# A compression network in a two-block transformer step: windows standing, weights moving, and its place behind two score steps

## What is computed

```python
kcc = compress_tokens(kc, pe[0], w1[0], b1[0], w2[0], b2[0])   # 15 windows of 32 tokens, 4 heads
vcc = compress_tokens(vc, pe[1], w1[1], b1[1], w2[1], b2[1])   # gelu(xb @ w1 + b1) @ w2 + b2
o_cmp = compressed_attention(q, kcc, vcc)       # 15 keys
o_sel = selected_block_attention(q, ks, vs, ...)  # at 256 tokens: all causal keys
o_win = banded_attention(q, kw, vw, 512, None)
o = g0 * o_cmp + g1 * o_sel + g2 * o_win ; y = o @ w_out
```

## Time and profile before

| what | time |
|---|---|
| median of 3 runs | 1802.1 us (1791.11 to 1802.98) |
| the profiled execution | 1789.85 us |
| its span (first to last instruction) | 1787.6 us |
| end of nsa_v to start of out2 | 1156.57 to 1261.03 us |

### The profile page before, as it was taken

The page is one execution under the profiler, slowest core; times in us unless marked ns, Lnnn a source line. Parts: engine busy times, 40 slices in busy tenths (PEclk is TensorE's granted clock), DMA queues, the critical chain, the costliest instruction groups (busy, mean ns, idle before and its releaser), DMA issues.

```text
span 1787.6 us, 32466 instructions
## 1 busy us (share of the span) xinstructions
PE 1694.1 (95%) x11348; PEld 1520.5 (85%) x11348; DVE 1216.1 (68%) x2234; ACT 916.6 (51%) x1749; POOL 565.1 (32%) x230
## 2 busy tenths in 40 slices
PE   2997999999999999999999999989899999799998
PEld 1985899999999998788888878976799999589997
DVE  5467509779718993878887758639578877646665
ACT  2445444455469994454545454247544445554443
POOL 0780377989975455000000007320210004130000
PEclk8899899999999999999999999969999998989999
DMA  8665455556653335888888655343568764136663
GB/s 324 224 207 169 144 177 176 178 185 178 185 168 118 113 111 183 326 283 291 293 290 285 195 165 149 120 150 126 165 224 282 281 224 133 34 107 188 188 187 107
DMA packets 98568, 341.14 MB, mean 191 GB/s; under 512 B 12290, under 2 KB 16146, under 8 KB 98482
## 3 DMA queue, kind: packets, MB, share of 16 engines
q1 hardware_dynamic: 94130, 336.01, 56.9%
q10 hardware_dynamic: 4352, 4.02, 0.8%
HBM read 337.87 MB, written 1.07 MB: 190 GB/s over the span
## 4 chain that ended last, share of the span: by engine, by line
PE 87%; DVE 5%; ACT 3%; DMA 3%; issue 2%; ACTq 0%; SPq 0%; DVEq 0%
PE banks L611 25%; PE banks L612 25%; PE banks L613 25%; PE banks L890 3%; DMA arena<-in_ada 2%; DVE arena L1546 1%; PE banks L1054 1%; PE banks L776 1%; DMA ada_ring<-in_ada 1%; PE banks L750 1%; PE banks L682 1%; PE banks L789 1%; DVE arena L1653 1%; PE banks L675 1%; DVE negmax L1632 1%
## 5 line engine op out<-in xcount | busy, mean ns | idle before, releaser
L564 POOL TENSOR_TENSOR weights_low<-ring,weights_high 128x1024 fp32r<-128x1024 f32 x226 | 564.9, 2512 | 1041.1 <-DVE ht_low L1621 625.9
L1167 ACT ACTIVATE weights_high<-ring 128x1024 fp32r<-128x1024 f32 x480 | 505.2, 1054 | 510.1 <-PE banks L613 481.2
L611 PE MATMUL banks<-ht_high,weights_high 128*128 128x256 f32 x2008 | 582.5, 290 | 8.5 <-DVE ht_low L1621 6.0
L612 PE MATMUL banks<-ht_low,weights_high 128*128 128x256 f32 x2008 | 572.2, 285 | 0.0
L613 PE MATMUL banks<-ht_high,weights_low 128*128 128x256 f32 x2008 | 572.0, 285 | 0.0
L611 PEld LDWEIGHTS banks<-ht_high,weights_high 128*128 128x128 f32 x2008 | 389.5, 194 | 14.2 <-issue 11.4
L612 PEld LDWEIGHTS banks<-ht_low,weights_high 128*128 128x128 f32 x2008 | 389.7, 194 | 2.7
L613 PEld LDWEIGHTS banks<-ht_high,weights_low 128*128 128x128 f32 x2008 | 389.1, 194 | 0.0
L1601 DVE TENSOR_TENSOR weights_low<-ring,weights_high 128x1024 fp32r<-128x1024 f32 x254 | 310.5, 1223 | 40.2 <-ACT weights_high L1167 34.5
L611 PE MATMUL banks<-weights_high,ga_parts 128*128 128x512 f32 x504 | 197.7, 392 | 5.8 <-DVE ga_parts L1903 5.8
L612 PE MATMUL banks<-weights_low,ga_parts 128*128 128x512 f32 x504 | 197.0, 391 | 0.0
(11 more groups left out here) (249 smaller groups left out, 2328.8 us busy)
## 6 DMA issues: line engine op xcount, KB each, us to landing
ring<-in_stream SPq DMA_DIRECT2D x490, 512.0 KB, 3.6
arena<-in_ada SPq DMA_DIRECT2D x88, 512.0 KB, 4.1
ada_ring<-in_ada SPq DMA_DIRECT2D x56, 512.0 KB, 4.3
arena<-bias_rows ACTq DMA_DIRECT2D x1, 2048.0 KB, 13.4
X<-in_x SPq DMA_DIRECT2D x1, 1024.0 KB, 5.8
out<-X SPq DMA_DIRECT2D x4, 256.0 KB, 2.0
arena<-arena ACTq DMA_DIRECT2D x8, 127.5 KB, 4.9
arena<-in_norm_final SPq DMA_DIRECT2D x1, 512.0 KB, 4.6
```

Of the source, the lines that this page charges most:

```text
L564: pool.tensor_tensor(WL[:, c % SLOTS, :], ring[:, c % SLOTS, :], WH[:, c % HIGHS, :], ALU.subtract)\
L611: pe.matmul(out, wh, xh, start=start, stop=False, **kw)
L612: pe.matmul(out, wh, xl, start=False, stop=False, **kw)
L1167: act.activation(WH[:, c % HIGHS, :], ring[:, c % SLOTS, :], ACT.Copy).then_inc(S["high_ready"], 1)
```

## The change

1. Phi's first layer is turned round: 60 window columns are stationary, 256 columns of `w1` move. Keys write partitions 0 to 59 and values partitions 64 to 123 of bank 7, alternately. The weights are reordered on the host so that a chunk holds 4 rows-of-128 with 256 columns each, keys and values in turn.
2. The bias is now a row, added by two matmuls with a row of ones. The gelu (60 x 256, twice) leaves hidden units on the free axis, so 4 transposes and one VectorE copy turn them back before the second layer.
3. Phi's first layer stands behind the scores of steps 0 and 1, the transposes behind step 0's, the second layer behind step 1's. In group 0 both "cmp" steps are moved behind the other four.
4. nsa_v goes to banks 6 and 7, out of the way of the scores; the gates on VectorE come after the windows.
5. SyncE loads the 8 chunks of out2 between ada pieces 1 to 8, no longer ahead of all of them; ScalarE's `high` of the first four stands in the last four attention steps (20 to 23), no longer right behind phi. The `low` of each on GpSimd follows.

```diff
-        att2 = plan(lambda g: ["sel", "win", "cmp"], 8, 8)
+        att2 = plan(lambda g: ["sel", "win", "cmp"], 8, 8, lambda s: (s["g"], s["g"] == 0 and s["last"]))
...
-            load_chunks(ahead + SLOTS, chunk["out2"] + SLOTS)
+            load_chunks(ahead + SLOTS, chunk["out2"])
...
+                if 1 <= i <= SLOTS:
+                    load_chunk(chunk["out2"] + i - 1)
...
+                if kind == "cmp":
+                    pe.wait_ge(S["cmp_taken"], 2)
...
+            def phi_hidden():
+                pe.wait_ge(S["windows_ready"], 4)
+                pe.wait_ge(S["phi_loaded"], 16 * 7)
+                pe.wait_ge(S["vv_taken"], 2)
+                for q in range(4):
+                    c = chunk["phi"] + 2 * q
+                    for kv in range(2):
+                        arrived(c + kv)
+                    for l in range(4):
+                        for kv in range(2):
+                            m = pe.matmul(banks[window_rows[kv], 7, 0:T], WIN[:, kv, 4 * q + l, :],
+                                          ring[:, (c + kv) % SLOTS, l * T:(l + 1) * T], start=q == 0 and l == 0, stop=False,
+                                          skip_group_check=True)
+                            if l == 3:
+                                m.then_inc(S["chunk_used"], 1)
+                pe.wait_ge(S["ones_row_ready"], 1)
+                for kv in range(2):
+                    m = pe.matmul(banks[window_rows[kv], 7, 0:T], ones_row[0:1, 0:60], A(A_B1R, 2, T)[0:1, kv, :],
+                                  start=False, stop=True, skip_group_check=True)
+                m.then_inc(S["phi_done"], 1)
+
+            def phi_turned():
+                pe.wait_ge(S["hid_ready"], 2)
+                for kv in range(2):
+                    r = window_rows[kv]
+                    if kv:
+                        pe.wait_ge(S["hid_turned"], 1)
+                    for mm in range(2):
+                        m = pe.transpose(banks[:, 7, T + (2 * kv + mm) * 60:T + (2 * kv + mm + 1) * 60],
+                                         HIDT[r, mm * P:(mm + 1) * P], ident[r, r])
+                    m.then_inc(S["hid_turned"], 1)
...
-            pe.wait_ge(S["gate_taken"], 1)
-            for kv in range(2):
-                pe.wait_ge(S["windows_ready"], 2 * (kv + 1))
...
-            attention(att2, keys2, lambda s, h: Q2[:, h // 2, :], vals2)
+            attention(att2, keys2, lambda s, h: Q2[:, h // 2, :], vals2, {-1: phi_hidden, 0: phi_turned, 1: phi_out})
...
+            def take_hidden(i):
+                if i == 1:
+                    act.wait_ge(S["phi_done"], 1)
+                    for r in window_rows:
+                        act.activation(HIDT[r, :], banks[r, 7, 0:T], ACT.Gelu_apprx_tanh).then_inc(S["hid_ready"], 1)
...
+            def beside_att2(i):
+                if i == 2:
+                    act.wait_ge(S["cmp_ready"], 1)
...
+                if i >= len(att2) - HIGHS:
+                    used(chunk["phi"] + 8 + i - len(att2))
...
+                if step == 1:
+                    dve.wait_ge(S["hid_turned"], 2)
+                    dve.tensor_copy(A(A_HID, 240), banks[:, 7, T:T + 240]).then_inc(S["hid_taken"], 1)
```

More of the change, by code:

```diff
@@ L793, in values, with attention @@
                 m.then_inc(S["values_done"], 1)
-            def attention(steps, keys, queries, vals):
+            def attention(steps, keys, queries, vals, beside={}):
                 for s in steps[:2]:
                     scores(s, keys, queries)
+                if -1 in beside:
+                    beside[-1]()
                 for i, s in enumerate(steps):
@@ L804, in attention @@
                     probs_transpose(s)
+                    if i in beside:
+                        beside[i]()
                 values(steps[-1], vals)
@@ L1036, in _ @@
             m.then_inc(S["gate_ready"], 1)
+            pe.wait_ge(S["out_taken"], OUTS["nsa"] + 16)
+            deep("nsa_v", 4, 512, per=2, bank=6)
+            def phi_hidden():
[18 more added lines that the diff above has]
+                m.then_inc(S["phi_done"], 1)
@@ new lines, in phi_out @@
+            def phi_out():
+                pe.wait_ge(S["hid_taken"], 1)
+                for mm in range(2):
+                    m = pe.matmul(banks[:, 7, 0:60], A(A_W2D, 2, P)[:, mm, :], HID[:, mm, :], start=mm == 0, stop=mm == 1)
+                for g in range(4):
+                    o = banks[0:N_CMP, 7, T + g * HD:T + (g + 1) * HD]
+                    for mm in range(2):
+                        pe.matmul(o, HID[:, 2 + mm, g * N_CMP:(g + 1) * N_CMP], A(A_W2, 2, 2, HD)[:, 1, mm, :],
+                                  start=mm == 0, stop=False)
+                    m = pe.matmul(o, ones[0:1, 0:N_CMP], A(A_B2V, HD)[0:1, :], start=False, stop=True)
+                m.then_inc(S["cmp_ready"], 1)
@@ L1230, in take_values, with attention @@
                     .then_inc(S["y_high_ready"], 1)
-            def attention(steps):
+            def attention(steps, first=lambda i: None, beside=lambda i: None):
                 exps(steps[0])
                 for i, s in enumerate(steps):
+                    first(i)
                     if i:
                         take_probs(steps[i - 1])
+                    beside(i)
                     if i > 1 and steps[i - 2]["last"]:
@@ L1678, in _ @@
             dve.memset(epsc[:], EPS).then_inc(S["eps_ready"], 1)
+            dve.memset(ones_row[:], 1.0).then_inc(S["ones_row_ready"], 1)
             dve.memset(one_of[:], 0.0).then_inc(S["one_ready"], 1)
```

76 lines of the change are left out of this document (22 added, 54 removed).

## The result

The changed kernel takes 1778.63 us (median of 13 runs, 1773.12 to 1785.98); the kernel before, run beside it, 1794.09 (13 runs, 1790.12 to 1802.98). The ratio is 0.9915 with an interval of 0.9900 to 0.9929, so the gain is 12.7 to 17.9 us, 15.5 by the medians. The forecast was 1781.5 us and a gain of 20.6. The time is 2.9 us from it, and that is partly luck: the 1802.1 us that it started from lay 8.0 us above the median of before that 13 runs give, and the gain was put 5.1 us too high, so the two errors took each other away in part. The forecast gave 0.55 to a gain beyond 1%; it came out at 0.85%, for which it had 0.40. The profiled executions are 1789.85 and 1779.83 us.

What follows compares the result with a forecast made beforehand. TensorE was busy 95% of the span, but VectorE's start and pace on the attention were taken to count. Gain 22.1 - 1.5 = 20.6 us from a median of 1802.1 gave 1781.5 us; range 1767 to 1793.

Steps and rivals of the forecast that it cites:

- a: Ahead of phi: two score steps of 128 keys take 2.0 us, so phi begins at 1158.5.
- b: Phi's first layer: halves run beside each other, 0.47 us a pair, 8.0 us in all; bounds 7.3 and 14.6.
- rival 1: Phi's first layer: the halves do not overlap, 14.6 us instead of 8.0; gain 14.0, time 1788.1; chance 0.13.
- rival 3: Small bare costs: phi's weight loads (3.4 us) or pauses at both table loads (2.6); gain 17.2 or 18.0; chance 0.08.
- c: From phi's end to group 1's first maxima: a chain of 16.3 us, gaining 22.1 us up to there.
- rival 2: Start is a chain at TensorE's lower clock, or the tail costs more: 8 us lost, gain 12.6; chance 0.20.
- d: The rest of the attention, from group 1 to out2, stays as it was at 56.1 us.
- e: The tail, steps 20 to 23: the moved `high` and `low` cost 1.5 us; bounds 0 and 13.1.
- f: Moved nsa_v banks, rotary wait, gates, bias row and out2's chunks cost nothing; 3.5 us once if cover were gone.
- Rival 4: Slower: phi at the lower clock without overlap takes 29.2 us, group 0 loses 8; time 1810.7; chance 0.04.

Runs made afterwards that it cites:

- fed kernel of before: The kernel before with 10 idle bf16 matmuls while TensorE waits for the gelu between phi's keys and values: 1787.74 us, ratio 0.9960.
- fed steps: The changed kernel with 2 idle bf16 matmuls in each attention step ahead of the wait for the probabilities: 1779.36 us, ratio 0.9927.
- filled run: The changed kernel with lows on VectorE, idle matmuls in attention steps and more in the last ones: 1776.18 us; with early highs and lows: 1777.46 us.
- phi first: The changed kernel with phi's first layer ahead of the two score steps: 1784.85 us, ratio 0.9950 to the kernel before.
- highs behind: The changed kernel with the four `high` behind the exponentials (steps 19 to 22) instead of ahead: 1779.67 us, ratio 0.9916.
- both of these: The changed kernel with the four `low` on VectorE and the four `high` behind the exponentials: 1785.11 us, ratio 0.9949.
- after again: The changed kernel run once more for a second profile, nothing edited: one run, 1774.4 us.
- halves apart: The changed kernel with phi's matmuls as four on the keys' partitions, then four on the values', not in turn: 1776.17 us, ratio 0.9908.

## Why the prediction was right, and where it was wrong

a. *Two score steps ahead*: 1.95 us for 2.0. Right. The place itself was worth 6 us with what hangs on it.

b. *Phi's first layer*: 7.7 us for 8.0 (1162.03 to 1169.73 with the bias). Mechanism and size were right: the two halves run beside each other, a pair of matmuls costs 0.43 us, and the 0.04 that I added to each pair from the values' row is not there. So rival 1 is answered by the trace: one half alone takes 0.43 us a matmul, and 32 of them one behind the other would be 13.8 us by that figure, hardly less than the 14.5 of before at the full clock (2 x 7.25). So turning the operands round pays here because it lets two halves be used, not by itself. (Before, 60 moving columns took 0.227 us a matmul, with the weight loads busy for 7.11 us beside 7.25 of matmuls; whether the loads set that pace no run shows.) Neither small cost of rival 3 was there: the loads lie under the matmuls, and no pause stands ahead of or behind the bare table load.

c. *From phi to group 1*: forecast 26.2 us behind nsa_v, measured 27.13, 25.86 again, 28.5 in four profiles of the same start, and 25.24 with the clock held. The sum of the chain fits; the clock's part was left out, up to 3.3 us. So rival 2's first half happened, at a quarter to four tenths of its price of 8. I had forecast a clock of 1.0 up to group 1; in the first profile it fell to 0.50 for 7 us or so ahead of it.

d. *The rest unchanged*: wrong by 1.7 us, plus 1.5 of clock in the first profile. Group 1 takes 18.35 to 18.57 us at a clock of 1.00 in three runs with the new order, and 16.89 in the fed kernel of before. The fed steps show where, in VectorE's timeline at the start of group 1:

```profile
1183.71 0.18 DVE L1683 RECIPROCAL rsum<-sums 128x4 f32<-128x4 f32 x1 [0.41 <-ACT arena L1238]
1185.58 0.69 DVE L1668 TENSOR_REDUCE negmax<-banks 128x4 f32<-128x512 f32 x1 [0.81 <-PE banks L768]
```

VectorE waits 0.41 us for exponentials and 0.81 for the next scores, so the second maxima come 2.97 us behind the first (1182.61); before it was 1.55 (1204.90 to 1206.45), with no wait. Both "cmp" steps of group 0 now stand right ahead of this place. That they are short and leave VectorE less to do while the others work is argued, as no run undid that order alone.

e. *The tail* is the step that failed: forecast 1.5 us, measured 4.9 in the first profile and 3.6 in the second. The mechanisms named are there. GpSimd holds VectorE up, in VectorE's timeline after:

```profile
1234.60 2.62 DVE L1684 TENSOR_SCALAR arena<-arena,rsum 128x15 f32<-128x15 f32 x4
1241.91 1.31 DVE L1682 TENSOR_TENSOR rsum<-rsum,arena 128x4 f32<-128x4 f32 x1
```

and in TensorE's, what it waits for, and how the last values run:

```profile
1237.27 1.03 PE L784 MATMUL banks<-const,arena 128*15 128x128 f32 x4 [2.52 <-DVE arena L1684]
1243.54 1.97 PE L797 MATMUL banks<-arena 128*64 128x128 f32 x16 [1.11 <-ACT arena L1247]
```

But four `high` and four `low` there cost 0.9 us once the clock is held and the lows are VectorE's. The other 4.0 and 2.7 are the clock and GpSimd's meetings with VectorE; how they share is not shown, as no filled run left the lows on GpSimd. What there is points to the clock as the larger part: it stood at 0.50 in a part of every tail that was not filled, in both orders, and taking the lows from GpSimd without holding the clock left the tail at 26.6 us. Rival 2 had named it ("the tail costs more"). What I left out is that the profile of before held a short such fall (0.92 over its last group) which another execution of nearly the same kernel had long (0.73, 25.62 us). Whether the new order makes it fall more often than the old is open: with one profile of each kernel I can't tell, and it may be that the true loss in e is nearer to the forecast than to 4.9.

f. *At nothing*: VectorE waited for one ada piece, 0.32 us under phi where it waited afterwards anyway, and phi did not wait for its chunks. Right.

So: forecast 22.1 - 1.5 = 20.6; in the first profile 21.20 - 3.14 - 4.94 = 13.12, in the second 22.47 - 1.73 - 3.62 = 17.12, and 12.7 to 17.9 by the runs. Of its own list of what would make it wrong one thing came, in both profiles: the last group over 26 us. Rival 4 didn't come: phi ran at 1.00. Two small slips of its sums changed nothing: the top of the range takes 10 us of gain for rival 2, which is put at 12.6 elsewhere, and 9 us of TensorE's work at the lower clock would cost 9, not about 8. The later start of the stage (3.5 us) can't be put down to the change: nsa_v ends anywhere from 1157.4 to 1163.9 in the profiles of the new order, and at 1156.6 and 1164.1 in the two of the old.

## What to carry to other kernels

When few rows meet many columns, let the few stand and the many move, and write the results of two independent products to the two halves of the partitions: 32 matmuls of 256 columns replaced 64 of 60 at half the price because they ran in pairs. Independent work put ahead of them covers what they wait for. An experiment that should keep two things apart has to be checked in the trace for whether it did: groups of four still overlapped. Small matmuls with waits around them are where the clock falls; before the cost of moved work is read from one profile, see how the same stretch varies over two, since here 3 to 4 us came and went with the clock alone. With the clock held, conversion work on ScalarE and VectorE cost less where the engines wait for each other anyway (0.9 us in the tail against 3.5 in VectorE's groups).

## What the runs showed of the hardware

- A plain fp32 matmul of 256 moving columns takes 0.43 us with 128 standing columns and with 60. Two with 60 that write partitions 0 to 59 and 64 to 123 take 0.43 us together. They need not alternate one by one: in groups of four matmuls (8 records), TensorE began the next group when the one before had 3 records still to start.
- A subtraction of 128x1024 on GpSimd (2.4 us) holds up some VectorE operations until it ends, by up to 2.1 us: sums of two operands in SBUF, and scalings (TENSOR_SCALAR). A RECIPROCAL from SBUF to SBUF that fell into it took its usual 0.18 us, and the L1682 right behind it 1.31 instead of 0.16. The subtraction is held up itself: begun 0.24 us behind an ada piece, one took 3.25 us.

```profile
1239.71 1.28 DVE L1577 SCALAR_TENSOR_TENSOR arena<-arena,csilu 128x1024 f32<-128x1024 f32 x1
1241.70 0.18 DVE L1678 RECIPROCAL rsum<-sums 128x4 f32<-128x4 f32 x1 [0.57 <-ACT arena L1233]
```

```profile
1239.95 3.25 POOL L570 TENSOR_TENSOR weights_low<-ring,weights_high 128x1024 fp32r<-128x1024 f32 x1 [3.17 <-ACT weights_high L1194]
```

  The Trainium skill (SBUF — State Buffer, SBUF: two separate sides) says that a VectorE operation with two inputs in SBUF, or in a mode that uses two ports, and a GpSimd operation lock one shared pair of ports: whichever starts first has it for its whole length, and the other waits. The trace agrees, 0.9 us over the usual 2.36 there and 2.1 the other way. Whether the scalings ran in such a mode no run shows.
- Idle matmuls in TensorE's waits kept the granted clock at 1.00 through one whole stage (the filled tail) and through another up to its tail, at a price of 0.4 us in group 2 (17.04 against 16.65); in two other runs with the same filling ahead of the tail it fell once each, in the start and in group 1. They gain nothing where VectorE is the bound.
- The pieces of a stretch take a few values and not any: groups 1 and 2 and the tail came out at 18.1, 19.3 and 27.5 to 27.9 us in three kernels with different edits (phi first, highs behind, both of these), and at 18.61, 16.65 and 26.2 in two others (after again, halves apart), each time with the same granted clocks in the two groups (0.87 and 0.86; 0.91 and 1.00).
